# Second attention of a Trainium2 kernel: each key head once, and its copy in the other half of the partitions

## The reference, cut to what matters

```python
def attn_inputs(h, w_qkv, g_q, g_k, n_kv, with_q=True):
    y = h @ w_qkv
    q = rmsnorm(y[..., :D_MODEL].reshape(bsz, t, n_kv, N_HEADS // n_kv, HEAD_DIM), g_q)
    kv = y[..., D_MODEL:]
    k = rmsnorm(kv[..., :kv_w].reshape(bsz, t, n_kv, HEAD_DIM), g_k)
    v = kv[..., kv_w:].reshape(bsz, t, n_kv, HEAD_DIM)
...
q, k, v = attn_inputs(h, w_in, gq, gk, n_kv)
q_c, k_c, v_c = attn_inputs(hc, w_in, gq, gk, n_kv, with_q=not last)
q = apply_rope(q, cos, sin)
k = apply_rope(k, cos, sin)
o = sliding_window_attention(q, k, v, k_c, v_c, sink)
x = x + gt1 * (o @ w_out)
```

## Time and profile before

| | us |
|---|---|
| median of 3 runs | 3401.39 (3395.29 to 3402.13) |
| profiled execution: span, first to last instruction | 3398.5 |
| profiled execution: own total | not listed apart from the runs |
| mean granted TensorE clock | 0.981 of 2.4 GHz |
| products of this stage, first matmul to the last result taken up | 2725.08 to 2810.36 |
| stage of the values, head sums to first scores | 2812.79 to 2835.35 |

### The profile page before, as it was taken

The page is one execution under the profiler, slowest core; times in us unless marked ns, Lnnn a source line. Parts: engine busy times, 40 slices in busy tenths (PEclk is TensorE's granted clock), DMA queues, the critical chain, the costliest instruction groups (busy, mean ns, idle before and its releaser), DMA issues. The chain is left out here.

```text
span 3398.5 us, 51546 instructions
## 1 busy us (share of the span) xinstructions
PE 3245.2 (95%) x18667; PEld 2817.4 (83%) x18667; DVE 2274.4 (67%) x4666; ACT 1339.8 (39%) x2016; POOL 1352.5 (40%) x739
## 2 busy tenths in 40 slices
PE   8988999999999999999899999999989999999999
PEld 6756799999999999999686667788878877668877
DVE  7753888989995888887785777655460067654440
ACT  3444133335554433333313774422231145743331
POOL 3014356666665422221230664222223322444433
PEclk9989999999999999999999999999999999999999
DMA  7502457778999999998455504122212141133322
GB/s 240 147 26 106 167 162 253 238 242 306 370 354 359 391 371 361 361 364 291 137 170 131 95 2 161 63 62 62 62 46 68 46 132 57 70 105 93 94 79 93
DMA packets 235080, 588.98 MB, mean 173 GB/s; under 512 B 52580, under 2 KB 113508, under 8 KB 230797
## 3 DMA queue, kind: packets, MB, share of 16 engines
q1 hardware_dynamic: 177644, 420.58, 37.9%
q0 software_dynamic: 36864, 134.23, 10.6%
q10 hardware_dynamic: 20384, 31.73, 2.6%
HBM read 529.03 MB, written 56.91 MB: 172 GB/s over the span
## 5 line engine op out<-in xcount | busy, mean ns | idle before, releaser
L445 POOL TENSOR_TENSOR ahead_low<-w_raw,ahead_high 128x1024 fp32r<-128x1024 f32 (+1 forms) x159 | 421.3, 2650 | 872.8 <-ACT ahead_high L381 872.7
L241 PE MATMUL psum<-h_high,ahead_high 128*128 128x512 f32 (+1 forms) x1384 | 493.3, 356 | 4.7 <-POOL ahead_low L445 4.7
L242 PE MATMUL psum<-h_low,ahead_high 128*128 128x512 f32 (+1 forms) x1384 | 490.3, 354 | 0.0
L243 PE MATMUL psum<-h_high,ahead_low 128*128 128x512 f32 (+1 forms) x1384 | 488.9, 353 | 0.0
L381 ACT ACTIVATE ahead_high<-w_raw 128x1024 fp32r<-128x1024 f32 (+1 forms) x159 | 178.0, 1120 | 739.1 <-PE psum L243 701.8
L2179 POOL TENSOR_TENSOR pick_u_low<-pick_u_raw,pick_u_high 128x1024 fp32r<-128x1024 f32 x128 | 306.9, 2398 | 210.0 <-ACT pick_u_high L2302 208.9
L241 PE MATMUL psum<-peer_h_high,pick_u_high 128*128 128x384 f32 x1024 | 353.0, 345 | 9.0 <-POOL pick_u_low L2179 9.0
L242 PE MATMUL psum<-peer_h_low,pick_u_high 128*128 128x384 f32 x1024 | 346.9, 339 | 0.0
L243 PE MATMUL psum<-peer_h_high,pick_u_low 128*128 128x384 f32 x1024 | 344.0, 336 | 0.0
L241 PEld LDWEIGHTS psum<-h_high,ahead_high 128*128 128x128 f32 x1384 | 259.8, 188 | 47.0 <-issue 5.0
L243 PEld LDWEIGHTS psum<-h_high,ahead_low 128*128 128x128 f32 x1384 | 260.9, 188 | 40.4
(11 more groups left out here) (439 smaller groups left out, 8170.4 us busy)
## 6 DMA issues: line engine op xcount, KB each, us to landing
pick_u_raw<-in_expert_uT SPq DMA_DIRECT2D x128, 512.0 KB
v_raw<-in_expert_v SPq DMA_DIRECT2D x128, 512.0 KB
mod_w<-in_w_mod SPq DMA_DIRECT2D x88, 512.0 KB, 3.8
w_raw<-in_ffn_up SPq DMA_DIRECT2D x84, 512.0 KB, 3.6
gelu_dram<-pick_gelu ACTq DMA_DIRECT2D x128, 192.0 KB
gates_dram<-gate_plane SPq DMA_DIRECT2D x24, 1024.0 KB
g<-gates_dram SPq DMA_DIRECT2D x31, 768.0 KB
w_raw<-in_ffn_down SPq DMA_DIRECT2D x29, 704.0 KB, 4.1
```

Source lines behind the costliest of these rows:

```text
L241: nc.tensor.matmul(bank, w_high, x_high, start=first, stop=False)
L242: nc.tensor.matmul(bank, w_high, x_low, start=False, stop=False)
L243: return nc.tensor.matmul(bank, w_low, x_high, start=False, stop=last)
L445: nc.gpsimd.tensor_tensor(w_low[r % 2][:, :, :], raw[r % n_raw][:, :, :], w_high[r % 2][:, :, :].bitcast(F32), ALU.subtract).then_inc(k.w_ ...
```

## The change

The weight layout gives each key head once: 2 key chunks, of two key heads each, and 8 query chunks, so 10 products. After chunks 0 and 1 are scaled, SyncE issues four transfers of 64 partitions x 768 tokens (two for each chunk, one in each direction) that put the copy of each head on the other half, at `KEY_CHUNKS + n`. TensorE waits for them behind the last step of the value product (`tensor`, s = 7). `key_of` picks the original or the copy. Groups are now of 2, 4 and 4 chunks; the first has 64 rows of factors. The orders written by hand are moved to match. Two helpers, `slot_of` and `fills`, keep count of slots. Left out below: `root`, `mean`, `refine` and `scale` (rows of the group in place of all rows, slots by `slot_of`) and counts of semaphores.

```diff
@@ -2680,6 +2680,9 @@
...
+KEY_CHUNKS = SWA_WIDTH // P
+
+
@@ -2688,7 +2691,8 @@
...
     def __init__(self, k, t, layer, b, ahead):
...
-        self.n_keys, self.n = KV_HEADS, KV_HEADS + KD
+        self.n_keys, self.n = KEY_CHUNKS, KEY_CHUNKS + KD
+        self.groups = [range(0, KEY_CHUNKS)] + [range(KEY_CHUNKS + i * GROUP, KEY_CHUNKS + (i + 1) * GROUP) for i in range(KD // GROUP)]
@@ -2703,7 +2707,7 @@
...
-        self.rows_raw = k.place("swa_rows_ahead", SWA_AT, 2 * D)
+        self.rows_raw = k.place("swa_rows_ahead", SWA_AT + 2 * D, 2 * D)
@@ -2722,7 +2726,22 @@
     def banks(self, n):
         if n < self.n_keys:
             return [self.k.psum[:, 2 * n + i, 0:m] for i, (_, m) in enumerate(PIECES)]
-        return [self.k.psum[:, n % GROUP, :]]
+        return [self.k.psum[:, (n - self.n_keys) % GROUP, :]]
+
+    def group_of(self, n):
+        return [n in g for g in self.groups].index(True)
+
+    def slot_of(self, n):
+        return n - self.groups[self.group_of(n)][0]
+
+    def fills(self, n):
+        return sum(self.slot_of(m) == self.slot_of(n) for m in range(n + 1))
+
+    def rows_of(self, g):
+        return slice(0, HEADS_AT_ONCE * len(self.groups[g]))
+
+    def key_of(self, half, g):
+        return self.b.key[HALVES[half], g // 2 if g % 2 == half else KEY_CHUNKS + g // 2, :]
@@ -2743,14 +2762,20 @@
 
     def factors_out(self, sp, g):
         sp.wait_ge(self.y_done.sem, self.y_done.at(g + 1))
-        sp.dma_start(self.factors[g].ap(), self.y[:, :]).then_inc(self.y_out.sem, 16)
+        rows, w = self.rows_of(g), self.width(self.groups[g][0])
+        sp.dma_start(self.factors[g].ap()[rows, 0:w], self.y[rows, 0:w]).then_inc(self.y_out.sem, 16)
+
+    def other_halves(self, sp):
+        sp.wait_ge(self.scaled.sem, self.scaled.at(self.n_keys))
+        for n in range(self.n_keys):
+            for to, source in (HALVES, HALVES[::-1]):
+                sp.dma_start(self.b.key[to, KEY_CHUNKS + n, :], self.b.key[source, n, :]).then_inc(self.rope_in.sem, 16)
 
     def spread(self, sp, g):
         sp.wait_ge(self.y_out.sem, self.y_out.at(16 * (g + 1)))
-        for j in range(GROUP):
-            n = GROUP * g + j
-            if g:
-                sp.wait_ge(self.scaled.sem, self.scaled.at(n - GROUP + 1))
+        for j, n in enumerate(self.groups[g]):
+            if g and j < len(self.groups[g - 1]):
+                sp.wait_ge(self.scaled.sem, self.scaled.at(self.groups[g - 1][j] + 1))
             for h in range(2):
                 sp.dma_start(self.slots[j][h * HEAD:(h + 1) * HEAD, 0:self.width(n)], bass.AP(self.factors[g], (HEADS_AT_ONCE * j + h) * TOK, [[0, HEAD], [1, self.width(n)]])
                              ).then_inc(self.spread_in[j].sem, 16)
@@ -2758,7 +2783,7 @@
     def take(self, act, n):
...
-        if n >= 2 * GROUP:
+        if n >= self.groups[2][0]:
@@ -2769,33 +2794,33 @@
...
     def sum(self, pe, g):
-        pe.wait_ge(self.squared.sem, self.squared.at(GROUP * (g + 1)))
-
-        pe.wait_ge(self.taken.sem, self.taken.at(self.n_keys))
+        group = self.groups[g]
+        pe.wait_ge(self.squared.sem, self.squared.at(group[-1] + 1))
...
-        for (t0, m), bank in zip(self.pieces(GROUP * g), self.sum_banks(g)):
-            for j in range(GROUP):
-                mm = self.nc.tensor.matmul(bank[HEADS_AT_ONCE * j:HEADS_AT_ONCE * (j + 1), :], heads, self.square_slot(GROUP * g + j)[:, t0:t0 + m], start=True, stop=True)
+        for (t0, m), bank in zip(self.pieces(group[0]), self.sum_banks(g)):
+            for j, n in enumerate(group):
+                mm = self.nc.tensor.matmul(bank[HEADS_AT_ONCE * j:HEADS_AT_ONCE * (j + 1), :], heads, self.square_slot(n)[:, t0:t0 + m], start=True, stop=True)
...
@@ -2835,18 +2860,16 @@
                 for n in range(4):
                     load(n + 6)
                     self.swap(sp, n)
-                for n in range(4, 6):
-                    load(n + 6)
-                    self.swap(sp, n)
+                self.swap(sp, 4)
+                self.factors_out(sp, 0)
+                self.swap(sp, 5)
+                self.spread(sp, 0)
                 self.swap(sp, 6)
-                self.factors_out(sp, 0)
+                sp.wait_ge(k.w_low.sem, k.w_low.at(2 * RING))
+                sp.dma_start(self.rows_raw[:, :], self.t["swa_v"][0]).then_inc(self.rows_in.sem, 16)
                 self.swap(sp, 7)
-                self.spread(sp, 0)
+                self.other_halves(sp)
                 self.swap(sp, 8)
-                sp.wait_ge(k.w_low.sem, k.w_low.at(2 * RING + 2))
-                sp.dma_start(self.rows_raw[:, :], self.t["swa_v"][0]).then_inc(self.rows_in.sem, 16)
-                self.swap(sp, 9)
-                self.swap(sp, 10)
                 self.factors_out(sp, 1)
 
             @block.scalar
@@ -2863,9 +2886,9 @@
                     if n + 2 < n_all:
                         round_weights(n + 2)
                     self.take(act, n)
-                    if n == 5:
+                    if n == 3:
                         self.root(act, 0)
-                    if n == 9:
+                    if n == 7:
                         self.root(act, 1)
 
             @block.gpsimd
@@ -2888,7 +2911,7 @@
...
-                        before = (n - self.n_keys) // 2 if n < 2 * GROUP else n - GROUP
+                        before = (n - self.n_keys) // 2 if n < self.n_keys + GROUP else n - GROUP
@@ -2896,29 +2919,29 @@
                             mm = split_product(nc, bank, w_high[n % 2][:, c, :], w_low[n % 2][:, c, :], k.h_high[:, c, t0:t0 + m], k.h_low[:, c, t0:t0 + m],
                                                c == 0, c == KD - 1)
                     mm.then_inc(k.product_done.sem, 1)
-                    if n == 4:
+                    if n == 2:
                         self.sum(pe, 0)
-                    if n == 8:
+                    if n == 6:
                         self.sum(pe, 1)
 
             @block.vector
             def _(dve):
                 negate_scale(k, dve, k.par("swa_gq"))
                 norm.vector(dve)
-                for n in range(4):
+                for n in range(self.n_keys):
                     self.rotate(dve, n)
                 self.mean(dve, 0)
+                self.rotate(dve, 2)
+                self.refine(dve, 0)
+                self.rotate(dve, 3)
                 self.rotate(dve, 4)
-                self.refine(dve, 0)
+                for n in range(self.n_keys):
+                    self.scale(dve, n)
                 self.rotate(dve, 5)
+                self.mean(dve, 1)
                 self.rotate(dve, 6)
-                for n in range(4):
-                    self.scale(dve, n)
+                self.refine(dve, 1)
                 self.rotate(dve, 7)
-                self.mean(dve, 1)
-                self.rotate(dve, 8)
-                self.refine(dve, 1)
-                self.rotate(dve, 9)
         for r in range(RING):
             k.weights_in[r].base += 16 * len(range(2 + (r - 2) % RING, n_all, RING))
         k.product_done.base += n_all
@@ -2951,34 +2974,32 @@
         self.sum(pe, 2)
 
     def tensor(self, pe, s):
-        pass
+        if s == KD - 1:
+            pe.wait_ge(self.rope_in.sem, self.rope_in.at(16 + 2 * 16 * self.n_keys))
 
     def vector(self, dve, s):
         if s == 0:
             self.mean(dve, 2)
-            self.rotate(dve, 10)
+            self.rotate(dve, 8)
         if s == 1:
             self.refine(dve, 2)
         if s == 3:
-            self.rotate(dve, 11)
-        if s == 4:
-            self.scale(dve, 4)
-            self.scale(dve, 5)
-        if s == 5:
-            self.scale(dve, 6)
-            self.scale(dve, 7)
+            self.rotate(dve, 9)
+        if s in (4, 5):
+            for n in self.groups[1][2 * (s - 4):2 * (s - 3)]:
+                self.scale(dve, n)
         if s == KD - 1:
-            for n in range(8, 12):
+            for n in self.groups[2]:
                 self.scale(dve, n)
 
     def count(self):
         for s, n in ((self.taken, self.n), (self.squared, self.n), (self.summed, 3), (self.mean_ready, 3), (self.y_ready, 3), (self.y_done, 3), (self.y_out, 48),
...
@@ -2987,7 +3008,7 @@
...
-    stage_rows(k, t["swa_v"], 1, SWA_WIDTH, ALL_TILES, lambda n, i: [(v[:, i, :], 0, SWA_WIDTH)], SWA_AT + D, (rotary,), 6, SWA_WIDTH, rotary.rows_in,
+    stage_rows(k, t["swa_v"], 1, SWA_WIDTH, ALL_TILES, lambda n, i: [(v[:, i, :], 0, SWA_WIDTH)], SWA_AT - D, (rotary,), 6, SWA_WIDTH, rotary.rows_in,
@@ -2999,7 +3020,7 @@
...
                 value = lambda j, lo=lo, hi=hi, g=g: v[:, lo + j if j < hi - lo else TILES + j - (hi - lo), g * HEAD:(g + 1) * HEAD]
-                pairs.append(Pair([b.q[h, q, i * P:(i + 1) * P] for h in HALVES], [[(b.key[h, g, lo * P:hi * P], m), (b.key[h, g, SEQ:TOK], CTX)] for h in HALVES],
```

(39 more changed lines are left out.)

## The result

The kernel before ran in 3398.34 us (median of 4 runs on the chip where the two were compared, 3391.91 to 3402.13), the changed one in 3379.57 (4 runs, 3376.81 to 3383.89): 18.8 us less, ratio 0.995 (95% interval 0.9936 to 0.9964). The forecast was 19.3 us less, on the median of 3401.39 that was known then. The profiled execution of the changed kernel took 3380.51 us, with a span of 3378.7.

The account below looks back on a forecast made before the run. TensorE's products were taken to bound the stage, VectorE and SyncE's queue the value stage. 16.86 + 0.72 + 0.78 + 0.9 = 19.3 us off the 3401.39 median gave 3382 us; the terms' ends gave 3381 to 3385, extended by rivals to 3375 and 3390.

Parts of the forecast that it names:

- Term 1: Products of the second attention's keys and queries: third and fourth key chunks go, 2 x 8.43 = 16.86 us less.
- B: Rival in the eight query chunks: TensorE starves waiting for split weights; 6 us slower, 3407 us; chance 0.03.
- Term 2: First head sums in the products' stage: 16 matmul records become 8, 0.72 us less.
- half of it: Step for the first head sums: half of their 1.50 us, less the overlap at its end, is saved, 0.72 us.
- Term 3: Products' end to value stage: ScalarE becomes last, the next stage starts 1.65 us behind the product, not 2.43; gain 0.78.
- Term 4: Value stage: spread of group 1 starts about 1.1 us earlier, last factors leave when ready; gain 0.9 us.
- The last factors leave when ready: Value stage: the last group's factors, sent at 2820.09 though ready at 2819.08, no longer wait for SyncE's queue; gain 0.9 us.
- rival C: Value stage shrinks to ScalarE's bound (2.09 instead of 0.9) and a low clock is missed: gain 21 to 22; chance 0.10.
- its own signs: Value stage: wrong if last factors leave over 6.5 us in, or group 1's spread later than 2.1; length about 21.7.
- The lower bound of term 4: Value stage: at 2.04 us each, four key copies hold the transfers for 8.2 us, a loss of 1.6.
- At nothing: TensorE's wait at the value product's last step, value rows' load, new memory places and attention: no cost, copies hidden.
- Rival A: Products' end: chain of swap, rotation and spread on busy VectorE takes over; gain only 14.1, time 3387 us; chance 0.17.

## Why the prediction came out

The sum was 19.3 us, and the mean of the three pairs of profiles gives 19.3 from the first product to the scores; both medians (18.8, 20.5) lie about it. That it came out so closely is luck: two of its terms were wrong in opposite directions, by -0.7 and +0.9, and the start of the program alone moves single runs by several us.

- **Term 1, two key chunks, 16.86:** right, 16.88, if the head sums gave nothing. From the second chunk's end the products last 47.31 or 47.32 in every run of the changed kernel's kind but the one with 2.77 us of head sums, and the clock is 1.00 from 2749 to 2793. No rival that lets TensorE wait (B) showed: no wait in the products, GpSimd at 16.71 of 44 us.
- **Term 2, head sums, 0.72:** wrong, 0.02 at most (1.50 against 1.48). The step that failed is "half of it": the records were counted, and not which columns of the array they use. The Trainium skill would have said so (TensorE: Matmul & The Clock Gate, "Part 3: Packing small matmuls — row/col tiling"): small matmuls at different tile positions of the array run at the same time. The runs agree, with 1.50, 1.48 and 2.77 us.
- **Term 3, the end of the products, 0.78:** right in kind, 0.95. ScalarE is last: the take ends 1.17 behind the last product, VectorE 1.45 ahead of it (I had 0.9 ahead), SyncE 0.44 ahead. The barrier costs 0.31 behind ScalarE, not the 0.47 read behind VectorE.
- **Term 4, the value stage, 0.9:** too small, 1.77, and its mechanism wrong. "The last factors leave when ready" happens (6.53, and 7.30, 6.65, 6.46 before), but is worth 0.27 and is not what the last spread waits for. That is the last rotation, whose swap seems slowed by the spread of group 1 (0.66), beside 0.49 for a clock that dipped in one of the three executions before, and 0.62 in the issue of the last spread. The part of rival C that expects a missed dip is in this term. One number under the term was an outlier: the spread of group 1 starting at 2.12. Its factors had taken 3.84 to land; in the two other profiles of before they took 2.57 and 2.56, and the spread started at 0.85 and 0.83. By its own signs the term was to be wrong if the last factors left more than 6.5 into the stage: they left at 6.52 and 6.53, and the stage was 1.2 to 2.2 shorter than the 21.7 it gave.
- **The lower bound of term 4**, 2.04 for each copy in a queue, didn't occur: four copies are issued in 2.51, 0.63 each, and leaving them out changed nothing. What they take on the DMA engines by themselves no run isolates, so the 4.0 us that the prediction estimates from the Trainium skill ("SBUF — State Buffer", "Door 1: The DMA port swizzle") stay untested.
- **At nothing:** TensorE's last-step wait and the attention behind it cost nothing that shows (scores to end: -0.5 of means that scatter by 2.4).
- **Rival A** was not seen: VectorE had 2.6 us to spare to ScalarE at the end of the products. The run with six multiplies puts its slack at 4.31 - 1.85 = 2.46, the same less the 0.16 by which the barrier costs more behind VectorE (0.47 against 0.31).

## What to carry to other kernels

A stage that TensorE bounds is worth its products, to a few hundredths; the estimate goes wrong at its edges. There, follow a chain through the program order of each engine and not through the data alone: here the last spread stood behind a rotation's swap, whose data it never reads. And count small matmuls by the fullest column group, and repeat the profile of both kernels before a difference of a microsecond is explained.

## What was not expected of the hardware

Eight matmul records and sixteen take the same 1.5 us when the sixteen use twice as many column groups. The same kernel with the same gap of 2.43 us had a dip of the clock in one execution and none in two others. A queue's issue of a transfer, 0.60 us otherwise, took 0.94 to 1.40 in four profiles where one 16 KB transfer of kind "instruction" was under way. And with no instruction changed, the time to the first product varies from 2717.2 to 2727.1 us over the runs, while a stretch of 47 us in which TensorE never waits repeats to 0.01.
